# Chunk 0's second half in another order, and chunk 1's rows transposed on TensorE

## The reference, cut to what matters

```python
h = _rmsnorm(x, norm_g)
u = jnp.einsum('btd,de->bte', h, w_in)
a_b, a_c, a_x, a_g, b_v, b_a, b_g, c_u, c_g, x_q, x_g = jnp.split(u, N_SPLITS, axis=-1)
y_a = a_b * _dwconv(concat(hist_a, a_c * a_x), conv_a_w) * silu(a_g)
z = _dwconv(concat(hist_b, b_v * sigmoid(b_a)), conv_b_w) + conv_b_bias
y_b = silu(_layernorm(z, ln_b_g, ln_b_b)) * silu(b_g)
y_c = (pool_mix(trailing_means(c_u) - c_u) + pool_bias) * pool_scale * silu(c_g)
y_x = softmax(q @ k.T / 8) @ v * silu(x_g)
y_prompt = _rmsnorm(x + concat(y_a, y_b, y_c, y_x) @ w_out, final_norm_g)
```

## Time and profile before

| what | us |
|---|---|
| median of 3 runs (1491.47 to 1492.65) | 1491.7 |
| the profiled execution's own time | 1492.88 |
| its span, first to last instruction | 1491.1 |
| TensorE matmul busy | 1436.1 (96%) |
| VectorE busy | 1182.1 (79%) |
| ScalarE busy | 564.5 (38%) |
| GpSimd busy | 217.1 (15%) |

### The profile page before, as it was taken

How to read it: one execution, slowest core, us unless ns; L and a number is a source line. 1 busy time by engine, 2 the same in 40 slices (tenths; PEclk the granted TensorE clock), 3 DMA queues, 4 the chain that set the end, 5 groups by cost and what they waited for, 6 DMA issues and landing times.

```text
span 1491.1 us, 32627 instructions
## 1 busy us (share of the span) xinstructions
PE 1436.1 (96%) x11742; PEld 1227.0 (82%) x11742; DVE 1182.1 (79%) x3098; ACT 564.5 (38%) x1242; POOL 217.1 (15%) x180
## 2 busy tenths in 40 slices
PE   5978899999999999999999999999999999999996
PEld 4767688888888888888888888888888888888884
DVE  6997695968869596978959596886959697895965
ACT  6773243323424233333334332333424332332423
POOL 0161011111111011111101111111101111110110
PEclk9989999999999999999999999999999999999998
DMA  9996535555553545564463555555364556445474
GB/s 271 254 322 217 210 97 200 182 212 197 165 229 105 219 168 183 197 225 174 132 252 116 205 177 211 197 175 218 112 228 152 183 197 225 181 138 215 130 248 160
DMA packets 129826, 286.26 MB, mean 192 GB/s; under 512 B 12553, under 2 KB 70589, under 8 KB 129789
## 3 DMA queue, kind: packets, MB, share of 16 engines
q1 hardware_dynamic: 129789, 285.77, 55.6%
HBM read 226.65 MB, written 59.08 MB: 192 GB/s over the span
## 4 chain that ended last, share of the span: by engine, by line
PE 90%; DMA 3%; DVE 2%; ACT 1%; issue 1%; POOL 0%; SPq 0%; ACTq 0%; DVEq 0%
PE u L532 21%; PE u L533 21%; PE u L534 21%; PE sps L532 5%; PE sps L534 4%; PE sps L533 4%; PE qps L532 4%; PE qps L534 4%; PE qps L533 4%; PE ops L613 2%; DMA ring<-wo_split 1%; PE sps L733 1%; DMA rows<-in_w_out 1%; PE u L669 0%; DVE z L1355 0%
## 5 line engine op out<-in xcount | busy, mean ns | idle before, releaser
L532 PE MATMUL u<-h_hi,w_hl 128*128 128x256 f16 (+1 forms) x2992 | 791.1, 270 | 17.0 <-DVE w_hl L1337 6.5
L533 PE MATMUL u<-h_lo,w_hl 128*128 128x256 f16 (+1 forms) x2992 | 790.2, 270 | 0.0
L534 PE MATMUL u<-h_hi,w_hl 128*128 128x256 f16 (+1 forms) x2992 | 789.8, 270 | 0.0
L1355 DVE SCALAR_TENSOR_TENSOR z<-glu,cst,z 128x256 f32<-128x256 f32 (+1 forms) x1020 | 423.0, 485 | 0.5
L532 PEld LDWEIGHTS u<-h_hi,w_hl 128*128 128x128 f16 x2992 | 293.8, 99 | 63.8 <-issue 8.1
L534 PEld LDWEIGHTS u<-h_hi,w_hl 128*128 128x128 f16 x2992 | 293.7, 99 | 33.7
L533 PEld LDWEIGHTS u<-h_lo,w_hl 128*128 128x128 f16 x2992 | 293.7, 99 | 33.2 <-issue 0.7
L880 ACT ACTIVATE gate<-u,inv 128x256 f32<-128x256 f32 (+1 forms) x204 | 82.7, 457 | 127.0 <-PE u L534 126.8
L1804 POOL TENSOR_TENSOR sa<-cu 128x540 f32<-128x540 f32 (+1 forms) x17 | 30.6, 1802 | 572.1 <-ACT cu L880 507.9
L532 PE MATMUL qps<-ring,y_hi 128*128 128x512 f32 x258 | 102.9, 399 | 2.8 <-DMA ring<-wo_split 2.8
L532 PE MATMUL sps<-ring,y_hi 128*128 128x512 f32 (+1 forms) x262 | 104.1, 397 | 0.8 <-DMA ring<-wo_split 0.4
(11 more groups left out here) (220 smaller groups left out, 1852.9 us busy)
## 6 DMA issues: line engine op xcount, KB each, us to landing
ring<-wo_split SPq DMA_DIRECT2D x256, 512.0 KB, 7.8
ob<-in_x_prompt SPq DMA_DIRECT2D x34, 512.0 KB, 4.1
probs_turned<-probs SPq DMA_DIRECT2D x130, 128.0 KB, 2.4
pt<-probs_turned SPq DMA_DIRECT2D x32, 512.0 KB, 3.4
out<-ob SPq DMA_DIRECT2D x32, 512.0 KB, 3.1
rows_turned<-rows SPq DMA_DIRECT2D x122, 128.0 KB, 2.4
w_hl<-in_w_in SPq DMA_DIRECT2D x20, 512.0 KB, 7.4
wo_split<-ring SPq DMA_DIRECT2D x16, 512.0 KB, 5.2
```

What stands on the lines that cost most here:

```text
L532: nc.tensor.matmul(out, a_hi, b_hi, start=first, stop=False)
L533: nc.tensor.matmul(out, a_hi, b_lo, start=False, stop=False)
L534: return nc.tensor.matmul(out, a_lo, b_hi, start=False, stop=last)
L1355: ins = nc.vector.scalar_tensor_tensor(z[:, c, 0:n], glu[:, c, k:k + n], w, z[:, c, 0:n], ALU.mult, ALU.add)
```

## The change

The order of slots, of SyncE's queue and of every engine's list for chunk 0 is rewritten from about the point at which the first attention scores are made. `b_g` and `w10` change places in `FIRST`, and four slots r0 to r3 are added for the transposed rows of chunk 1, which TensorE now writes itself (`next_rows`); ScalarE and VectorE split them from PSUM (`next_rows_hi`, `next_rows_lo`). The two row transfers through DRAM of chunk 0 are gone. Both inverse roots of chunk 1's rows are made in one go (`both_rms`), on two columns.

```diff
@@ -56,7 +56,7 @@
 FIRST = ["w0", "w1", "w2", "b_a", "b_v", "w3", "x_q", "w4", "w5", "w6", "c_u", "w7", "w8", "a_c", "a_x",
- "w9", "a_b", "a_g", "b_g", "w10", "c_g", "mix", "x_g", "zf", "zb"]
+ "w9", "a_b", "a_g", "w10", "b_g", "c_g", "mix", "x_g", "zf", "zb", "r0", "r1", "r2", "r3"]
@@ -270,6 +270,7 @@
            "x_g": (xg_ok, 1), "zb": (zs_ok, 1)}
+EMPTIED["r0"] = (row_lo_ok, 1)
 EMPTIED |= {f"w{g}": (wscl_ok, 3 * g + 1) for g in range(NG)}
@@ -378,7 +379,7 @@
         sp.dma_start(dst[0, 0].rearrange("(t p) h d -> p t (h d)", p=P), kv[:, :, off:off + GW]).then_inc(kv_in.sem, 16)
-    for p in range(RAW, PIECES):
+    for p in range(RAW, 11):
         keep(p - RAW)
@@ -400,9 +401,9 @@
     def row_across(i, t, m):
-        sp.wait_ge(row_t_ok.sem, row_t_ok.at(i, t + 1))
+        sp.wait_ge(row_t_ok.sem, row_t_ok.at(i, t + 1 - 2))
         put_out(rows_turned[t], turned[t], m, rows_out[t])
-        sp.wait_ge(rows_out[t].sem, rows_out[t].at(i, 16 * (m // SQ)))
+        sp.wait_ge(rows_out[t].sem, rows_out[t].at(i, 16 * (m // SQ) - 64))
         take_back((xb, xp)[t], rows_turned[t], m, rows_in[t])
@@ -432,6 +433,9 @@
         probs_leave(0, 0, N)
+        for p in range(11, PIECES):
+            keep(p - RAW)
+            load_piece(p)
         for p in range(PIECES - RAW, PIECES):
@@ -439,12 +443,8 @@
         residual(0, N, x_here)
-        for q in range(RING, PIECES - 2):
+        for q in range(RING, PIECES):
             ring_load(0, q)
-        row_across(0, 0, P)
-        for q in range(PIECES - 2, PIECES):
-            ring_load(0, q)
-        row_across(0, 1, P)
         sp.wait_ge(row_lo_ok.sem, 1)
@@ -714,6 +714,17 @@
         ins.then_inc(ktp.sem, 1)
+
+    def next_rows(t, rows):
+        pe.wait_ge(x_scaled.sem, 4 + t + 1)
+        for h in range(2):
+            name = f"r{2 * t + h}"
+            pe.wait_ge(*emptied(0, name))
+            _, bank = slot(0, name)
+            for k in range(4):
+                c = (4 * h + k) * P
+                ins = nc.tensor.transpose(bank[:, k * P:(k + 1) * P], rows[:, c:c + P], ident[:, :])
+            ins.then_inc(u_ready.sem, 1)
@@ -770,16 +781,23 @@
         project(0, N, "a_g")
+        weight_sums(10)
         scores(0, N, 1)
         project(0, N, "b_g")
-        weight_sums(10)
         project(0, N, "c_g")
-        attend(0, N, 0)
         mix(0, N)
         project(0, N, "x_g")
+        out_begin(0, N)
+        out_pieces(0, N, 0, 4)
+        attend(0, N, 0)
+        attend(0, N, 1)
+        out_pieces(0, N, 4, Z_AT)
         z_rows(0, N)
-        attend(0, N, 1)
-        out_project(0, N)
+        out_pieces(0, N, Z_AT, PIECES - 2 * CT)
+        z_back(0, N)
+        next_rows(0, xb)
+        out_pieces(0, N, PIECES - 2 * CT, PIECES)
+        next_rows(1, xp)
@@ -905,12 +923,20 @@
     def row_hi(i, j, t, m):
-        act.wait_ge(rows_in[t].sem, rows_in[t].at(i, 16))
+        act.wait_ge(rows_in[t].sem, rows_in[t].at(i, 16 - 16))
         n_xg, _ = slot(i, "x_g")
...
             ins = nc.scalar.activation(h_hi[:, :, r0:r0 + SQ], src, ACT.Copy)
+        ins.then_inc(row_hi_ok.sem, 1)
+
+    def next_rows_hi(t):
+        for h in range(2):
+            n, bank = slot(0, f"r{2 * t + h}")
+            act.wait_ge(u_ready.sem, n)
+            ins = nc.scalar.activation(h_hi[:, 4 * h:4 * h + 4, t * P:(t + 1) * P],
+                                       bank[:, :].rearrange("p (k c) -> p k c", k=4), ACT.Copy)
         ins.then_inc(row_hi_ok.sem, 1)
@@ -1123,49 +1149,51 @@
         w_square(19)
-        piece_hi(1)
+        act.wait_ge(wsq_ok.sem, 20)
+        w_square(20)
+        w_square(21)
         scaled_out(0, N, "a_c", gate[:, 1, :, 0:N], ACT.Copy, ac_ok)
         w_high(15)
-        for k in range(2, 5):
-            piece_hi(k)
+        piece_hi(1)
         w_high(16)
+        piece_hi(2)
+        w_high(17)
+        piece_hi(3)
+        exps(0, N, 0)
+        w_high(18)
+        piece_hi(4)
+        w_high(19)
         piece_hi(5)
-        exps(0, N, 0)
-        for k in range(6, 8):
-            piece_hi(k)
-        w_high(17)
-        piece_hi(8)
-        w_high(18)
-        piece_hi(9)
-        w_square(20)
-        piece_hi(10)
-        w_square(21)
-        piece_hi(11)
+        probs_hi(0, N, 0)
+        w_high(20)
+        piece_hi(6)
+        w_high(21)
         d_high(0, N)
-        probs_hi(0, N, 0)
-        piece_hi(12)
-        w_high(19)
-        for k in range(13, 15):
+        for k in range(7, 9):
             piece_hi(k)
...
         scaled_out(0, N, "a_g", gate[:, 2, :, 0:N], ACT.Silu, ag_ok)
-        piece_hi(15)
         exps(0, N, 1)
-        for k in range(20, 22):
-            w_high(k)
+        for k in range(9, 11):
+            piece_hi(k)
         probs_hi(0, N, 1)
+        for k in range(11, 13):
+            piece_hi(k)
         b_gate(0, N)
+        y_high(0, N, 0, ya[:, :, 0:N], ya_ok)
+        piece_hi(13)
+        c_gate(0, N)
         mixed(0, N)
-        y_high(0, N, 0, ya[:, :, 0:N], ya_ok)
-        c_gate(0, N)
+        for k in range(14, 16):
+            piece_hi(k)
         scaled_out(0, N, "x_g", gate[:, 2, :, 0:N], ACT.Silu, xg_ok)
...
         y_high(0, N, 2, z[:, :, 0:N], yb_ok)
-        row_hi(0, *nxt[0])
-        row_hi(0, *nxt[1])
+        next_rows_hi(0)
+        next_rows_hi(1)
         out_squares(0, N, nxt[1][0])
@@ -1250,7 +1278,7 @@
-    def rsqrt(s, i, k, sq, v, w, y, mul, add=EPS):
+    def rsqrt(s, i, k, sq, v, w, y, mul, add=EPS, skip=0):
@@ -1270,7 +1298,9 @@
                 else:
-                    nc.vector.scalar_tensor_tensor(y[:, e], w[:, e], 1.5, y[:, e], ALU.add, ALU.mult).then_inc(s.sem, 1)
+                    more = skip if (r, c) == (2 * NEWTON - 1, cols - 1) else 0
+                    nc.vector.scalar_tensor_tensor(y[:, e], w[:, e], 1.5, y[:, e], ALU.add,
+                                                   ALU.mult).then_inc(s.sem, 1 + more)
@@ -1278,8 +1308,13 @@
-    def rows_scale(j, t, m, gain=gx, rows=xb):
-        dve.wait_ge(x_v.sem, RSQRT * (j + 1))
+    def both_rms(j):
+        dve.wait_ge(x_sq.sem, j + 2)
+        dve.wait_ge(x_scaled.sem, j)
+        rsqrt(x_v, 0, RSQRT * j, X_SQ, X_V, X_SH, X_Y, 1.0 / D, skip=2 * RSQRT - (4 + 4 * NEWTON))
+
+    def rows_scale(j, t, m, gain=gx, rows=xb, after=1):
+        dve.wait_ge(x_v.sem, RSQRT * (j + after))
         nc.vector.scalar_tensor_tensor(rows[0:m, :], rows[0:m, :], X_Y[0:m, t:t + 1], gain[0:m, :],
@@ -1301,6 +1336,14 @@
             ins = nc.vector.tensor_tensor(h_lo[:, :, r0:r0 + SQ], src, h_hi[:, :, r0:r0 + SQ], ALU.subtract)
+        ins.then_inc(row_lo_ok.sem, 1)
+
+    def next_rows_lo(t):
+        dve.wait_ge(row_hi_ok.sem, t + 1)
+        for h in range(2):
+            _, bank = slot(0, f"r{2 * t + h}")
+            o = (slice(None), slice(4 * h, 4 * h + 4), slice(t * P, (t + 1) * P))
+            ins = nc.vector.tensor_tensor(h_lo[o], bank[:, :].rearrange("p (k c) -> p k c", k=4), h_hi[o], ALU.subtract)
         ins.then_inc(row_lo_ok.sem, 1)
@@ -1574,41 +1617,35 @@
         w_low(15)
-        taps(0, N, 21, 22)
+        w_scale(9)
+        w_low(16)
         pool_diff(0, N)
-        w_low(16)
-        w_scale(9)
+        w_low(17)
         softmax_rcp(0, N, 0)
+        w_scale(10)
         conv_a_taps(0, N)
-        taps(0, N, 22, 23)
-        w_low(17)
+        probs_lo(0, N, 0)
         ab_out(0, N)
-        probs_lo(0, N, 0)
+        for k in range(18, 20):
+            w_low(k)
+        d_low(0, N)
         softmax_max(0, N, 1)
-        w_low(18)
-        taps(0, N, 23, 24)
-        w_low(19)
-        taps(0, N, 24, 25)
         ya_out(0, N)
-        d_low(0, N)
-        w_scale(10)
-        softmax_rcp(0, N, 1)
         for k in range(20, 22):
             w_low(k)
+        softmax_rcp(0, N, 1)
+        taps(0, N, 21, 23)
         probs_lo(0, N, 1)
-        taps(0, N, 25, 31)
+        taps(0, N, 23, 31)
+        yx_out(0, N)
         z_stats(0, N)
-        yx_out(0, N)
         z_norm(0, N)
-        rows_rms(*nxt[0])
-        rows_scale(*nxt[0])
-        row_turn(0, *nxt[0])
+        both_rms(nxt[0][0])
+        rows_scale(*nxt[0], after=2)
         yb_out(0, N)
-        rows_rms(*nxt[1])
         rows_scale(*nxt[1], rows=xp)
-        row_turn(0, *nxt[1])
-        row_lo(0, *nxt[0])
-        row_lo(0, *nxt[1])
+        next_rows_lo(0)
+        next_rows_lo(1)
         add_half(0, N, 0)
@@ -1826,10 +1863,13 @@
         windows(0, N)
-        for k in range(0, 16):
+        for k in range(0, 13):
             piece_lo(k)
         y_low(0, N, 0, ya[:, :, 0:N], 0)
+        piece_lo(13)
         yc_out(0, N)
+        for k in range(14, 16):
+            piece_lo(k)
         y_low(0, N, 4, yc[:, :, 0:N], 1)
```

## The result

The changed kernel takes 1504.9 us (median of 4, 1504.45 to 1506.65) against 1491.9 for the kernel before in the same session: ratio 1.0086, 95% interval 1.0074 to 1.0098. It is slower by 0.9%, in the direction of the forecast, but by 13 us where 5.3 were forecast. The profiled execution took 1504.89 us, its span 1503.1, 12.0 more than in the earlier trace rows.

What follows compares the result with a forecast made beforehand. TensorE is nearly always busy after chunk 0, so chunk 1's start decides: 6.8 us later, less 1.4 of restart, +5.4, 1498.3 for the profiled execution, 1497.1 against the median, stated as 1497.0; range 1489.5 to 1503.0.

Steps and rivals of the forecast that it cites:

- What bounds the kernel: TensorE is busy 1233.5 of 1235.0 us from 165 to 1400, so only chunk 1's start, 159.8 us before, matters.
- The front: Chunk 0 up to b_g, which waits for the bank freed by `ab_out`: ended at 99.3 us, bounds 96.0 and 102.6.
- half of the disturbance would go: VectorE ahead of `ab_out`: GpSimd's disturbance taken as 6.6 us, half of it lost with 5 low halves instead of 10.
- The rival in which all of it goes: At `ab_out`, 7.6 us of GpSimd disturbance go instead of 3.3: no change, 1492.7 us; chance 0.27 with mixtures.
- the term for the trip of the probabilities: SyncE's sends, 1.8 us to issue and 1.9 to land: first landed at 108.3, second returned at 134.0.
- its upper bound of 136: Return of the probabilities for the second `attend`: 136 us if load and return both take 5.4.
- The tail: From z's normalisation to chunk 1: transposes hidden in a gap, waits of 3.4 and 2.2 us, chunk 1 at 166.6.
- The clock did not stay up: Rival at the restarts of b_g, x_g, piece 4 and piece 12: no gap lowers the clock, 1487.9 us; chance 0.13.
- Pieces late too: Rival in the raw-buffer loop: nothing given back at `ab_out` (+3.3), loads of 5.4 us, 1502.8 us; chance 0.15.

Runs made afterwards that it cites:

- rows_only2: The kernel before with only chunk 1's rows transposed on TensorE, lists in the old order, repeated with more executions: 1484.2 us, ratio 0.995.
- order_only: The changed kernel with its new lists, but chunk 1's rows turned and sent through DRAM as before: 1507.5 us, ratio 1.011.
- ab_first: The changed kernel with VectorE's `ab_out` ahead of `probs_lo(0)`: 1505.5 us, ratio 1.0107.
- leave_early: The changed kernel with load 10 and what follows it moved behind the first sends of probabilities in SyncE's queue: 1502.2 us, ratio 1.0066.
- both_sends: The changed kernel with load 10 onward behind the first probability sends and the second sends ahead of the last two writes, in SyncE's queue: 1500.6 us, ratio 1.0055.
- rows_only: The kernel before with only the transposes of chunk 1's rows on TensorE, ahead of output pieces 6 and 12, lists as before: 1484.3 us, ratio 0.995.
- mended: The changed kernel with both probability sends earlier in SyncE's queue, `z_rows` straight behind the attends, and row transposes among the pieces: 1490.6 us, ratio 0.9994.

## Why the prediction was right and wrong

*What bounds the kernel* held: from 171 to 1400 us TensorE is busy for all but 2.5 us, and what chunk 0 lost came through. Of the span's +12.0, the start of chunk 1 makes 10.9 (forecast 6.8) and its restart gives back 0.9 (forecast 1.4). The last 2 us fell in the loop, where waits for ring pieces from 260 us on are 2.5 us in six places (L532) against 1.2 in two before; `rows_only2` has 0.5 and `order_only` 1.2, so they come and go between kernels; why they do, and where the rest of the 2 us is, stays open.

*The front* held. `ab_out` ended at 98.8 (forecast 99.3, bounds 96.0 and 102.6), b_g waited 6.96 us for it and started at 98.9. That half of the disturbance would go was a choice, and it is borne out: the nine `w_low` mean 1.44 us against 1.66, and 1.28 without GpSimd beside them. The rival in which all of it goes fails twice: `ab_out` did not come at 96, and `ab_first`, where b_g starts at 96.4, gains nothing, so an early `ab_out` would not have given the 4.3 us either. What disturbance is left can be seen further on, in the second `probs_lo`, beside GpSimd's low halves of pieces 12 to 15:

```profile
118.35 4.74 DVE L1422 SCALAR_TENSOR_TENSOR prow<-probs,st,prow 128x256 f16<-128x256 f32 x4
115.80 1.69 DVE L1379 SCALAR_TENSOR_TENSOR prow<-probs,st,prow 128x256 f16<-128x256 f32 x4
```

The second line is the same four operations before, where GpSimd had no piece left to do. By the Trainium skill, "SBUF — State Buffer", "Who interferes with whom", a VectorE operation with two inputs in SBUF and a GpSimd operation that reads SBUF exclude each other for a whole instruction; 3.05 us on four operations are about two of GpSimd's 1.45 each, so here the trace agrees in kind; at `ab_out`, where the rule taken at its full price would have given 96 or less, it does not.

***The failed step* is the term for the trip of the probabilities, both times.** The forecast gave each 1.8 us to issue and 1.9 to land, from a trip ahead of which the queue had issued nothing for 8 us, and by its own working put a load right ahead of the first sends and a return right ahead of the second. The first: sends began at 104.0 (forecast 104.6 by its working), landed at 110.1 (108.3). b's gate came 1.2 late, and x_g started at 119.3 (118.1). The second: sends began at 127.9 where the working gave 126.2. What held them was GpSimd. ScalarE made y_a's high half right behind b's gate, until 119.8, and from there GpSimd worked without a pause and ended the last low half at 127.0 (forecast 125.6):

```profile
119.87 1.49 POOL L1827 TENSOR_TENSOR y_lo<-ya,y_hi 128x512 fp32r<-128x512 f32 x1 [0.32 <-ACT y_hi L1012]
121.32 1.47 POOL L1832 TENSOR_TENSOR ring<-rows,ring 128x512 fp32r<-128x512 f32 x1
122.74 1.46 POOL L1861 TENSOR_TENSOR yc<-yc,gate 128x512 f32<-128x512 f32 x1
124.28 2.71 POOL L1832 TENSOR_TENSOR ring<-rows,ring 128x512 fp32r<-128x512 f32 x2
```

So the 1.2 us that the first trip was late by came through to the second sends; `leave_early` shows it from the other side, with the gate 1.9 us earlier and the second sends 1.9 earlier. Piece 15's load was 1.05 late as well, but its high half was ready at 124.2 and GpSimd came to it only at 125.5. The other 0.2 are GpSimd's own, and 0.3 more is the issue of the last write (at 127.02; the two writes shown as 1.75 us take 0.32 each) and of the return: 1.7 in sum. Then the issue of the sends took 2.3 and the landing 3.2. Sum 1.7 + 0.5 + 1.3 = 3.5: the return was back at 137.3, not 134.0, since it landed 0.2 sooner than counted. The mechanism (sends behind all the writes, only four pieces ahead of both attends) was right, its size was 3.8 us of waiting where 1.6 were forecast, and its upper bound of 136 was too low, for it varied the times of loads and return and not the trip. Behind it all keeps its distance: piece 4 at 141.7 (137.7), `z_back` at 155.7 (152.1), piece 12 at 160.4 (156.5), chunk 1 at 170.7 (166.6). The 0.7 added at piece 4 is the second `attend`, 1.49 us at half clock where 0.8 was taken. With the sends early, 2.4 (`leave_early`) and 5.6 us (`both_sends`) of chunk 1's start come back.

*The tail* held in its parts: `next_rows(0)` 1.04 us in the gap, 3.28 and 2.06 of waiting (3.4 and 2.2). Of the price in "TensorE: Matmul & The Clock Gate", "Part 4: PE-mode transpose", of the Trainium skill (transposes do not count as busy for the clock in the same way) the trace shows this: piece 12 restarts at 0.63 over 4.56 us, a loss of 1.7 us, between the 1.3 taken and the 2.6 by that rule. The gap is a wait of 3.3 behind transposes of 1.0, so the row does not separate them; in `rows_only`, with the transposes amid pieces, the clock stayed at 1.00.

*The rivals.* The clock did not stay up at b_g, x_g or piece 4. "Pieces late too", 1502.8, is the nearest in number and partly in kind (loads and writes late around piece 15), but its other term, `ab_out` at 102.6, did not occur. The forecast of 1497.0 was 7.9 us short. Of these 4.1 are the late start of chunk 1, 0.5 its restart, 2.0 the loop, and 1.2 were taken off because the profiled execution before lay that much over its median, which the one after does not. The range ended at 1503.0, 1.9 short: it held the unknown of `ab_out` and none for the trip, and +2 in the loop was not in it. The direction was no luck: the waits came where they were drawn. The loop's 2.0 us were in no term.

What the forecast did not ask is why the order was worse at all; the runs say it. Rows alone waits 12.7 us in chunk 0's second half, the new order 28.4: it takes away the waits for weights (6.5) and the wait for rows was gone by the other half of the change, but it makes b_g, x_g, the second `attend` and piece 4 wait for things at the end of long chains through ScalarE, GpSimd and one queue. Of the 20 us that it costs over rows alone, the edits of `mended` give back 14; the 6 that stay were not taken apart.

## What to carry to other kernels

When a change has two independent halves, run each alone first: here one half gained 7 us and the other lost 16. The longest wait in the table need not be on the path (2.9 of the 7 us at b_g went, and nothing was gained); ask what the engine behind it waits for next. And take a DMA trip's time from a row in which the same kind of transfer was issued just ahead of it in the queue; where there is none, give the term a range of its own.

## What was not expected of the hardware

- The same four sends of 128 KB took 1.77 to 1.80 us to issue in all 12 trips ahead of which the queue had issued nothing for 2.0 us or more, and 2.33 to 3.00 in all 14 with a transfer of 256 or 512 KB issued at most 0.8 us ahead. The DMA share does not tell them apart: the first trip of the kernel before was quick at a share of 0.94 (0.98 in the 2 us ahead), the first of the kernel after slow behind 2 us at 0.02.
- SyncE's issue of a single transfer of a piece, 0.32 to 0.55 us between 91 and 106.9 us and again between 115 and 119 us of the kernel after, took 1.12, 1.29 and 1.88 us between 106.9 and 111.3, one write behind the first sends.
- Eight 128x128 float32 transposes take 1.04 us on TensorE, and among products they left the granted clock at 1.00 (`rows_only`, two runs of eight between 137 and 152 us).
